# A hybrid encoder layer on one core: order of the projection jobs, first w in halves, low parts of w_out on GpSimd

## The reference

```
h    = rmsnorm(x) ; q, k, v, xr, gate = split(h @ w_in)      # 512,128,128,512,512
q, k = rope2d(rmsnorm(q)), rope2d(rmsnorm(k)) ; attn = softmax(q k / 8) v    # 8 heads, 2 kv heads
xc   = conv4(xr) + b
for d in (forward, backward):                                # gates by 64x64 blocks
    r, i = sigmoid(xc @ Wr + br), sigmoid(xc @ Wi + bi)
    a = exp(-8 r softplus(-lambda)) ; h_d = scan(a, sqrt(1 - a^2) * i * xc)
x    = x + concat(attn, (h_fwd + h_bwd) * gelu(gate)) @ w_out
x    = x + expert_choice_moe(rmsnorm(x))                     # 16 experts, 64 tokens each per sequence
```

## Time and profile before

| | us |
|---|---|
| median of 3 runs (lowest, highest) | 1080.12 (1079.93, 1083.85) |
| the profiled execution | 1081.51 |
| its span, first to last instruction | 1079.7 |

### The profile page before, as it was taken

How to read it: one execution, slowest core, us unless ns; L and a number is a source line. 1 busy time by engine, 2 the same in 40 slices (tenths; PEclk the granted TensorE clock), 3 DMA queues, 4 the chain that set the end, 5 groups by cost and what they waited for, 6 DMA issues and landing times.

```text
span 1079.7 us, 14786 instructions
## 1 busy us (share of the span) xinstructions
PE 991.9 (92%) x4935; PEld 824.2 (76%) x4935; DVE 813.7 (75%) x1030; ACT 708.3 (66%) x931; POOL 336.0 (31%) x190
## 2 busy tenths in 40 slices
PE   3999999978899999934999999999999999999995
PEld 3789997866766788833788888888888888888874
DVE  5658789867798322263898889988898889888883
ACT  6367767566798211141898777877797778877773
POOL 0000040065366000041064346533663356413320
PEclk9999999999999999966999999999999999999997
DMA  6111101000301543386899999999999999999851
GB/s 247 51 45 45 44 13 40 1 1 1 117 1 61 197 155 118 117 318 233 312 381 387 386 393 399 383 390 393 390 392 383 386 392 403 385 383 373 310 167 28
DMA packets 75232, 248.95 MB, mean 231 GB/s; under 512 B 9356, under 2 KB 16568, under 8 KB 75192
## 3 DMA queue, kind: packets, MB, share of 16 engines
q1 hardware_dynamic: 70584, 231.64, 56.0%
q0 software_dynamic: 4608, 16.78, 6.2%
HBM read 231.63 MB, written 16.78 MB: 230 GB/s over the span
## 4 chain that ended last, share of the span: by engine, by line
PE 77%; DVE 10%; ACT 7%; issue 3%; DMA 1%; SPq 0%; POOL 0%; ACTq 0%; POOLq 0%
PE bank L934 23%; PE bank L936 23%; PE bank L935 23%; PE bank L940 5%; DVE e_lo L1460 2%; ACT e_hi L865 2%; PE bank L1094 1%; PE bank L1057 1%; PE bank L1058 1%; ACT prob L825 1%; DMA x_nat<-in_x_prompt_dram 1%; DVE probT_lo L1398 1%; DVE row_stat L1386 1%; DVE top_idx L1445 1%; ACT probT_hi L818 1%
## 5 line engine op out<-in xcount | busy, mean ns | idle before, releaser
L934 PE MATMUL bank<-e_hi,xsT_hi 128*128 128x512 f32 x512 | 201.7, 394 | 1.6 <-DVE xsT_lo L1465 1.4
L936 PE MATMUL bank<-e_hi,xsT_lo 128*128 128x512 f32 x512 | 199.8, 390 | 0.0
L935 PE MATMUL bank<-e_lo,xsT_hi 128*128 128x512 f32 x512 | 199.8, 390 | 0.0
L639 POOL COPY idx_now<-idx_all 128x1 uint32 (+1 forms) x16 | 157.0, 9811 | 28.1 <-DMA y_dram<-ys,idx_now 28.1
L865 ACT ACTIVATE e_hi<-raw_gate 128x1024 fp32r<-128x1024 f32 x128 | 134.6, 1060 | 35.3 <-PE bank L936 33.8
L1460 DVE TENSOR_TENSOR e_lo<-raw_down,e_hi 128x1024 fp32r<-128x1024 f32 x128 | 146.9, 1220 | 2.4 <-ACT e_hi L865 0.6
L1460 DVE TENSOR_TENSOR e_lo<-raw_up,e_hi 128x1024 fp32r<-128x1024 f32 x128 | 146.7, 1219 | 1.4 <-ACT e_hi L865 1.3
L1460 DVE TENSOR_TENSOR e_lo<-raw_gate,e_hi 128x1024 fp32r<-128x1024 f32 x122 | 141.2, 1219 | 4.6 <-ACT e_hi L865 4.6
L865 ACT ACTIVATE e_hi<-raw_up 128x1024 fp32r<-128x1024 f32 x128 | 126.4, 1055 | 1.7 <-PE bank L936 0.3
L865 ACT ACTIVATE e_hi<-raw_down 128x1024 fp32r<-128x1024 f32 x128 | 125.2, 1060 | 1.1 <-PE bank L936 0.9
L934 PEld LDWEIGHTS bank<-e_hi,xsT_hi 128*128 128x128 f32 x512 | 96.5, 189 | 22.3 <-DVE xsT_lo L1465 1.8
(11 more groups left out here) (217 smaller groups left out, 2086.4 us busy)
## 6 DMA issues: line engine op xcount, KB each, us to landing
raw_gate<-in_exp_w_gate_dram SPq DMA_DIRECT2D x64, 1024.0 KB, 10.7
raw_up<-in_exp_w_up_dram SPq DMA_DIRECT2D x64, 1024.0 KB, 8.3
raw_down<-in_exp_w_down_dram SPq DMA_DIRECT2D x64, 1024.0 KB, 7.1
w_raw<-in_w_in_dram SPq DMA_DIRECT2D x7, 1024.0 KB, 5.2
wo_raw<-in_w_out_dram SPq DMA_DIRECT2D x8, 512.0 KB, 4.3
y_dram<-x SPq DMA_DIRECT2D x8, 512.0 KB, 5.5
h_rows<-h SPq DMA_DIRECT2D x8, 512.0 KB, 3.3
x_nat<-in_x_prompt_dram SPq DMA_DIRECT2D x4, 512.0 KB, 5.9
```

Source lines behind the costliest of these rows:

```text
L639: pool.tensor_copy(idx_now[:, 2:3], idx_all[:, bass.ds(e, 1)] if not isinstance(e, int) else idx_all[:, e:e + 1]).then_inc(idx_copied, 1)
L934: pe.matmul(out, l_hi, r_hi, start=first, stop=False)
L935: pe.matmul(out, l_hi, r_lo, start=False, stop=False)
L936: return pe.matmul(out, l_lo, r_hi, start=False, stop=last)
```

## The change

Eight first jobs: the order becomes (0,0) (0,1) (1,0) (1,1) for sequence 0, then the same channel tiles for sequence 1, where it was all of group 0 and then all of group 1. Jobs 0, 1 and 4 are issued as two halves of 24 products 256 wide (half the tokens each); jobs 2 and 3 as two parts of 12 products 512 wide (half the contraction each), between the x blocks of sequence 1. w group 0 comes in two loads of 512 KB, ahead of x blocks 2 and 3, and is split in two; w group 1 has a buffer of its own (`w1_raw`) and is loaded behind x block 3. The vector rows come after that, and go through bank 3. The step of an x block is cut into `square_x`, `norm_x`, `turn_x`, `hi_x`, `lo_x`.

Recurrence: c is 5, 9, 12, 16 for the four tiles, so conv, gates, decay and scan of tiles 0 and 1 are two jobs later than before and those of tiles 2 and 3 one. The splits of w groups keep the jobs 4, 8, 12 and so on, except that group 2 comes at job 6.

Tables: `load_tables` waits for two convs, not four, and stands one group earlier in SyncE's list. Rotations wait for bd_lo of all tiles too. The twelve early wo_lo are issued by GpSimd, with a semaphore of their own, in the same slots.

```diff
@@ -118,6 +118,7 @@
     x_nat = at("x_nat", R3, [P, NB, D], F32)
     g1b = at("g1b", SM + 16 * K, [P, D], F32)
     x_norm = at("x_norm", SM + 20 * K, [P, 2, D], F32)
+    w1_raw = at("w1_raw", SM + 32 * K, [P, KC, GW], F32)
...
-    ORDER = [(g, j) for g in range(3) for j in range(JOBS)]
+    ORDER = [(g, 2 * half + j) for half in range(2) for g in range(2) for j in range(2)]
+    ORDER += [(2, j) for j in range(JOBS)]
...
-    steps = [("sum_squares", 0)]
-    for b in range(NB + 1):
-        steps.append(("normalise", b))
-        if b == BPS - 2:
-            steps.append(("w_hi", 0))
-        if b == BPS - 1:
-            steps += [("w_lo", 0), ("vectors",)]
-        if b in (BPS - 1, BPS + 1):
-            steps.append(("project", (b - BPS + 1) // 2))
+    HALF = S // 2
+    steps = [("square_x", 0), ("norm_x", 0), ("square_x", 1), ("norm_x", 1), ("turn_x", 0), ("turn_x", 1),
+             ("hi_x", 0), ("lo_x", 0), ("w_hi", 0, 0), ("w_lo", 0, 0), ("hi_x", 1), ("lo_x", 1), ("w_hi", 0, 1), ("w_lo", 0, 1),
+             ("project_half", 0, 0)]
+    for b in range(2, BPS):
+        steps += [("square_x", b), ("norm_x", b), ("turn_x", b)]
+        if b == 2:
+            steps.append(("project_half", 1, 0))
+    steps += [("hi_x", 2), ("lo_x", 2), ("vectors",), ("hi_x", 3), ("lo_x", 3), ("project_half", 0, 1), ("project_half", 1, 1),
+              ("w_hi", 1), ("w_lo", 1)]
+    for i, b in enumerate(range(BPS, NB)):
+        steps += [("square_x", b), ("norm_x", b), ("project_part", 2 + i // 2, i % 2), ("turn_x", b)]
+        if i:
+            steps += [("hi_x", b - 1), ("lo_x", b - 1)]
+        if i == 2:
+            steps += [("empty", 0), ("empty", 1)]
+    steps += [("project_half", 4, 0), ("hi_x", NB - 1), ("lo_x", NB - 1), ("project_half", 4, 1), ("empty", 2), ("empty", 3)]
     steps.append(("softplus",))
     LRU_AT = {}
     for ct in range(CT):
-        c = 3 + 4 * ct
+        c = (5, 9, 12, 16)[ct]
         for n, step in ((c + 1, ("gates", ct, 0)), (c + 2, ("gates", ct, 1)), (c + 3, ("decay", ct)),
                         (c + 3, ("conv", ct + 1)), (c + 4, ("scan", ct))):
             if step != ("conv", CT):
                 LRU_AT.setdefault(n, []).append(step)
-    LRU_AT.setdefault(3, []).append(("conv", 0))
+    LRU_AT.setdefault(5, []).append(("conv", 0))
...
-        if n >= 2:
+        if n >= 5:
             steps.append(("project", n))
         first = [step for step in LRU_AT.get(n, []) if step[0] in ("scan",)]
         steps += first
-        if n:
+        if n >= 5:
             steps.append(("empty", n - 1))
-        for w in range(1, NG):
-            if n == max(FIRST_OF[w - 1], LAST_OF[w - 2] + 1 if w >= 2 else 0):
+        for w in range(2, NG):
+            if n == max(FIRST_OF[w - 1], LAST_OF[w - 2] + 1):
...
-        for b in range(NB):
+        def load_x(b):
             src = (x0 if b < BPS else x1)[0, (b % BPS) * P:(b % BPS + 1) * P, :]
             sp.dma_start(x_nat[:, b, :], src).then_inc(x_loaded[b], 16)
-            if b == 0:
-                sp.dma_start(g1b[:, :], norm1_g[0:1, :].to_broadcast([P, D])).then_inc(g1_loaded, 16)
-            if b == 1:
-                for at_row, rows_in in rows:
-                    sp.dma_start(vec_rows[at_row:at_row + rows_in.shape[0], :], rows_in).then_inc(vec_loaded, 16)
-            if b == BPS - 2:
-                load_w(0)
+
+        load_x(0)
+        sp.dma_start(g1b[:, :], norm1_g[0:1, :].to_broadcast([P, D])).then_inc(g1_loaded, 16)
+        load_x(1)
+        first = w_in[0, :, GROUPS[0][2]:GROUPS[0][2] + GW].rearrange("(k p) n -> p k n", p=P)
+        for part in range(2):
+            ks = slice(part * KC // 2, (part + 1) * KC // 2)
+            sp.dma_start(w_raw[:, ks, :], first[:, ks, :]).then_inc(w0_loaded[part], 16)
+        for b in range(2, BPS):
+            load_x(b)
+        sp.dma_start(w1_raw[:, :, :], w_in[0, :, GROUPS[1][2]:GROUPS[1][2] + GW].rearrange("(k p) n -> p k n", p=P)).then_inc(w1_loaded, 16)
+        for at_row, rows_in in rows:
+            sp.dma_start(vec_rows[at_row:at_row + rows_in.shape[0], :], rows_in).then_inc(vec_loaded, 16)
+        for b in range(BPS, NB):
+            load_x(b)
         sp.wait_ge(pool_ready, 5)
         load_bd(0)
         def load_tables():
 
-            sp.wait_ge(xc_done, CT)
+            sp.wait_ge(xc_done, 2)
             sp.dma_start(cos_sin[:, 0, :, :], rope_cos.rearrange("(b p) d -> p b d", p=P)).then_inc(tabs_loaded, 16)
             sp.dma_start(cos_sin[:, 1, :, :], rope_sin.rearrange("(b p) d -> p b d", p=P)).then_inc(tabs_loaded, 16)
             for i, g in enumerate((q_norm_g, k_norm_g)):
                 sp.dma_start(gains[:, 2 * i, :], g[0:1, :].to_broadcast([P, HD])).then_inc(tabs_loaded, 16)
 
-        for g in range(1, NG):
-            sp.wait_ge(wlo_done, g)
+        for g in range(2, NG):
+            if g == 2:
+                sp.wait_ge(w0_lo_done, 2)
+            else:
+                sp.wait_ge(wlo_done, g - 1)
             load_w(g)
             if 1 <= g - 1 < CT:
                 sp.wait_ge(bd_lo_done, g - 1)
                 load_bd(g - 1)
-            if g == NG - 2:
+            if g == 4:
...
-            elif kind == "split_lo" and n >= 2 * WO_EARLY:
+            elif kind == "split_lo" and n < 2 * WO_EARLY:
+                k, cols = n // 2, slice(n % 2 * D // 2, (n % 2 + 1) * D // 2)
+                pool.wait_ge(wo_hi_done, n + 1)
+                pool.tensor_tensor(wo_lo[k][:, cols], wo_raw[k][:, cols], wo_hi[k][:, cols].bitcast(F32), ALU.subtract).then_inc(wo_lo_pool, 1)
+            elif kind == "split_lo":
...
+            elif kind == "project_half":
+                n, half = arg
+                seq, j = divmod(ORDER[n][1], 2)
+                pe.wait_ge(ht_lo_done, BPS * (2 * seq + half + 1))
+                if n >= 4:
+                    pe.wait_ge(*evacuated(n - 4))
+                tok, ch = slice(half * HALF, (half + 1) * HALF), slice(j * P, (j + 1) * P)
+                for k in range(KC):
+                    if half == 0 and n == 0 and k % 4 == 0:
+                        pe.wait_ge(w0_lo_done, k // 4 + 1)
+                    src = slice(seq * S + half * HALF, seq * S + (half + 1) * HALF)
+                    ins = product(bank[:, n % 4, tok], w_hi[:, 0, k, ch], w_lo[:, 0, k, ch], hT_hi[:, k, src], hT_lo[:, k, src],
+                                  k == 0, k == KC - 1)
+                if half:
+                    ins.then_inc(proj_done, 1)
+            elif kind == "project_part":
+                n, part = arg
+                j = ORDER[n][1]
+                pe.wait_ge(wlo_done, 1)
+                ch = slice(j * P, (j + 1) * P)
+                for k in range(part * KC // 2, (part + 1) * KC // 2):
+                    ins = product(bank[:, n, :], w_hi[:, 1, k, ch], w_lo[:, 1, k, ch], hT_hi[:, k, 0:S], hT_lo[:, k, 0:S],
+                                  k == 0, k == KC - 1)
+                if part:
+                    ins.then_inc(proj_done, 1)
...
-                pe.wait_ge(wo_lo_done, 2 * (k + 1))
+                if k < WO_EARLY:
+                    pe.wait_ge(wo_lo_pool, 2 * (k + 1))
+                else:
+                    pe.wait_ge(wo_lo_done, 2 * (k - WO_EARLY + 1))
...
                 dve.wait_ge(tabs_done, 13)
+                dve.wait_ge(bd_lo_done, CT)
...
-                dve.wait_ge(xr_out, JOBS * (ct // 2) + 3 + ct % 2)
+                dve.wait_ge(xr_out, ORDER.index((ct // 2, 2 + ct % 2)) + 1)
...
-            elif kind == "split_lo":
-                if n < 2 * WO_EARLY:
-                    split_wo_lo(n // 2, n % 2)
```

More of the change, by code:

```diff
@@ L700, in _ @@
             kind, arg = step[0], step[1:]
[L701 to L714 removed]
+            if kind == "square_x":
+                b, = arg
+                act.wait_ge(x_loaded[b], 16)
+                act.activation(junk[:, :], x_nat[:, b, :], ACT.Square, accum_out=sumsq1[:, b:b + 1]).then_inc(sumsq_ready, 1)
+                act.wait_ge(sumsq_ready, b + 1)
+                act.activation(root1[:, b:b + 1], sumsq1[:, b:b + 1], ACT.Sqrt, scale=1.0 / D, bias=eps).then_inc(root_ready, 1)
+            elif kind == "hi_x":
+                b, = arg
+                for h in range(2):
+                    act.wait_ge(xt_done, 2 * b + h + 1)
+                    act.activation(hT_hi[:, 4 * h:4 * h + 4, b * P:(b + 1) * P],
+                                   bank[:, 4 + 2 * (b % 2) + h, :].rearrange("p (k t) -> p k t", k=4), ACT.Copy).then_inc(ht_hi_done, 1)
+            elif kind == "w_hi" and len(arg) == 2:
+                part = arg[1]
+                ks = slice(part * KC // 2, (part + 1) * KC // 2)
+                act.wait_ge(w0_loaded[part], 16)
+                act.activation(w_hi[:, 0, ks, :], w_raw[:, ks, :], ACT.Copy).then_inc(w0_hi_done, 1)
@@ L1256, in _ @@
             kind, arg = step[0], step[1:]
-            if kind == "normalise":
+            if kind == "norm_x":
                 b, = arg
-                def empty_turned(b):
```

(44 more changed lines are left out.)

41 lines of the change are left out of this document (15 added, 26 removed).

## The result

The changed kernel takes 1084.94 us (median of 20 runs, 1083.28 to 1088.47), the kernel before 1080.34 in as many runs (1078.44 to 1084.52): ratio 1.0042, 95% interval 1.0032 to 1.0053, so 4.6 us slower. The profiled executions stand at 1084.68 (span 1082.9) and 1081.51 (span 1079.7): +3.2 there.

What follows compares the result with a forecast made beforehand. The recurrence chain through VectorE and ScalarE was taken to pace each tile as much as TensorE. Terms +6.5 + 1.0 - 2.5 = +5.0 on the profiled 1081.5 gave 1086.5, in median terms 1085; range 1073 to 1090.5.

Steps and rivals of the forecast that it cites:

- step 4: Tile 2 one job sooner: gates(2,0) waits 4.7 us to 121.1, lru_out(2) at 159.9; moving costs and gains the chain nothing.
- step 5: Rotations and w_lo 5 after the first sum take 16.2 us: job 20 at 176.1, against 169.9 before.
- step 7: Clock drop after two new standstills on the chain, ahead of gates(1,1) and (2,1): 0 to 3.2 us, taken as 1.0.
- step 8: Early wo_lo on GpSimd, attention's second half: -2.5 taken, ceiling 3.5 us; at the disturbed price 1 to 3 lost.
- Step 1: Earlier start: first half product at 15.0 instead of 24.8, job 4 ends at 52.3, before 59.2; lead 6.9 us.
- Step 2: Recurrence moves two jobs back: gates(0,1) end at 74.2 against 70.3, so the chain starts 3.9 us late.
- Step 3: Splits of w 3 and w 4 fall into the recurrence chain: 2.7 us per tile, twice; lru_out(0) at 100.7.
- the splits hide: Rival, not slower: w 3 and w 4 fit beside the chain as before; 1080, with the clock kept 1078; chance 0.19.
- TensorE keeps its lead: Rival, faster: products pace the whole recurrence stage, job 20 at 160.2, 9.7 sooner; time 1071; chance 0.15.
- inside the same span: TensorE's wait of some 3.8 us at 161.7 for gates(3,0)'s sigmoids, held to lie within the 16.2 us before job 20.
- The early tables are worth nothing: Loading rotation tables earlier gains nothing, as they already ended before VectorE's first rotation; could cost 0.5 us beside scan 1.
- Step 6: From w_lo 5 to the first row_stat again 50.2 us: row_stat at 226.3, +6.5 us; possibly +2 or +9.

Runs made afterwards that it cites:

- e_tabs_late: The changed kernel with the rotation tables loaded as before, behind the conv of all four tiles: 1089.39 us, ratio 1.0082.
- h_sooner_squares: g_job_sooner with the square of q and k's block 1 behind gates(3,0) on ScalarE, not ahead of it: 1087.04 us, ratio 1.0052.
- c_splits: The changed kernel with the splits of w groups 3 and 4 one job earlier, ahead of the second gates: 1079.10 us, ratio 0.9983.
- f_sums_behind: d_c1317 with squares, sums and rotations of the first four blocks one job later too: 1086.29 us, ratio 1.0054.
- d_c1317: The changed kernel with tiles 2 and 3 back at one job later (c = 5, 9, 13, 17): 1094.49 us, ratio 1.0118.
- a_wo_dve: The changed kernel with the twelve early wo_lo back on VectorE, nothing else: 1088.58 us, ratio 1.0073.
- b_before_pool: The kernel before with only the twelve early wo_lo moved to GpSimd: 1076.37 us, ratio 0.9954.
- g_job_sooner: The changed kernel with the recurrence of tiles 0 and 1 a job sooner, w 3 and 4 splits behind the scans: 1086.40 us, ratio 1.0055.

## Why the prediction was right

The time (1085 forecast, 1084.94 measured) was right, and so was the chain of the recurrence behind it up to scan 2. The moral of step 4, the path and the tables of step 5, the place of step 7 and the size of step 8 were not, and that the time came out to 0.1 us is luck, as the sum at the end shows.

- *Step 1* (start at 15.0, job 4's end at 52.3): 14.43, and 51.63, where the first product of job 5 starts. The gap of 1.9 us was 1.71, and a turn held TensorE 0.79 us and not 0.96. What it left out: the start is not the same in each profile, as above. The drop of the clock behind the gap, which step 1 held possible, is there in *e_tabs_late* and *h_sooner_squares* (granted clock 0.75 and 0.74 in 26 to 29 us, 1.00 in the changed kernel's profile); it cost 1.5 us there, where step 1 had up to 1.3.
- *Step 2* (gates(0,1) end at 74.2): 73.8.
- *Step 3* (two splits in the chain, 2.7 each): lru_out(0) ends at 100.2, forecast 100.7; gates(1,1) at 101.5, forecast 102.1. *c_splits* measured 3.0 and 2.2. Its rival "the splits hide" set its own test, gates(2,0) before 118.5: it was 120.99. "TensorE keeps its lead" asked for gates(1,1) at 100, which was 1.5 us off, and for job 20 at 160.2, which came at 176.7.
- *Step 4* (gates(2,0) waits 4.7 us to 121.1, scan 2's lru_out at 159.9): 4.92, 120.99 and 159.8. The stop of over 2 us ahead of gates(2,1) was 0.29 only: the products at the low clock filled the time. Its "costs nothing, gains nothing" holds only with the rotations moved along (*f_sums_behind*). In the code as it stands, the moved scan passes two blocks of rotations in VectorE's queue, and this was worth 9.5 us (*d_c1317*). I had followed the chain and not asked what else shares the queue with the moved step.
- *Step 5* (job 20 at 176.1, for w_lo 5): 176.71, but not for w_lo 5, which was done at 175.78; TensorE did not stop there. The path ran through what step 5 had put "inside the same span": the 3.75 us ahead of gates(3,1), and 14 products at the low clock behind them (165.95 to 171.29), which brought TensorE to job 20 0.9 us behind w_lo 5. Two paths ended within a microsecond, and the time of the one was forecast by the other. "The early tables are worth nothing" was wrong. I had looked at the tables against the old place of the rotations; with conv 3 8.7 us later, as scan 2 is by 8.2, and the first sum no longer waiting 1.81 us, late tables would have been late. *e_tabs_late* shows VectorE waiting 1.32 us for them; to the first row_stat that is 1.8 us in the profiles, and 4.4 by the medians. The 0.5 us that step 5 held possible beside scan 1 is there (a product by xc at 132.68 took 1.73 us and not 1.22), but VectorE waited 3.69 us for ib behind it.
- *Step 6* (row_stat 226.3): 226.45.
- *Step 7* (clock +1.0, for the stops ahead of gates(1,1) and (2,1)): behind gates(1,1) the clock stayed up. It was low from 121 to 127 us, behind the stop ahead of gates(2,0), but there ib of tile 2 waited for lru_out for another 3.93 us, so this cost nothing. It was low again from 165 to 171, and these are the 0.9 us of step 5. At most 0.4 of them reached the attention: from the end of w_lo 5 to the first row_stat 50.7 us passed here and 50.2 in *c_splits*, where job 20 started at the end of w_lo 5. So the term of 1.0 beside step 6 wasn't there; up to 0.4 us of it are inside the 6.7.
- *Step 8* (-2.5): the attention lost 3.2 us in the profile, 3.6 (*a_wo_dve*) and 3.9 (*b_before_pool*) in the medians. The term was too small; my ceiling of 3.5 was reached, and passed by 0.4 in one pair of medians. The undisturbed prices held (1.294 and 1.296 us for the two kinds of subtraction, 0.699 for a prob, where 1.29 and 0.70 were used). That GpSimd is busy 37.46 of 40.80 us, where 37.3 was worked out, says less than it seems: the window holds 41 operations and not 39, and their times add to 39.3 us, since GpSimd's spans overlap. By the rule of the Trainium skill (SBUF — State Buffer, "SBUF: two separate sides") the disturber leaves with the edit; this case agrees, 1.296 us without VectorE's wo_lo and 1.471 with it.

The sum against the profiled execution was +5.0, of 6.5, 1.0 and -2.5; measured +3.2, of 6.7, 0 and about -3.2, and 0.3 won behind the attention. So the sum was 1.8 us too high: 1.0 in the clock, 0.7 in the attention and 0.3 behind it, less 0.2 in the way to the attention. The forecast time came out closer because the profiled execution of before lay 1.2 us over the median of its 20 runs and that of after 0.3 under, which made +4.6 between the medians.

## What to carry to other kernels

An earlier start is worth only what the slowest chain behind it can take up: list what each queue holds between two links of that chain, and put shared work (a split, a rotation) where the chain waits and before the point where the fast engine needs it. When a step moves, look at every queue for what it now passes and what now passes it; both large surprises here (9.5 us in *d_c1317*, 8 to 10 us against the forecast in *g_job_sooner*) were a step that now stood ahead of one that others were waiting for, on VectorE. Time parts of a bundle by themselves: one part gave 3.9 us, the rest took 8.5.
